# A chunked RWKV-7 recurrence: A turned by plain transpositions, and the transposed inverse turned over by TensorE and copied by ScalarE

## The reference, cut to what matters

```python
def rwkv7_scan(r, decay, k, v, kk, a):
    def step(S, inp):
        r_t, w_t, k_t, v_t, kk_t, a_t = inp
        sa = jnp.einsum('bhij,bhj->bhi', S, -kk_t)
        S = (S * w_t[:, :, None, :] + sa[..., None] * (kk_t * a_t)[:, :, None, :]
             + v_t[..., None] * k_t[:, :, None, :])
        return S, jnp.einsum('bhij,bhj->bhi', S, r_t)
```

## Time and profile before

| | us |
|---|---|
| median of 3 executions | 2356.2 |
| lowest, highest | 2354.84, 2357.73 |
| the profiled execution | 2356.96 |
| its span on the core | 2353.5 |
| outside the span | 3.5 |
| the stage's four pairs, from the first `prod` to the last `y` | about 220 |

### The profile page before, as it was taken

How to read it: one execution, slowest core, us unless ns; L and a number is a source line. 1 busy time by engine, 2 the same in 40 slices (tenths; PEclk the granted TensorE clock), 3 DMA queues, 4 the chain that set the end, 5 groups by cost and what they waited for, 6 DMA issues and landing times.

```text
span 2353.5 us, 36980 instructions
## 1 busy us (share of the span) xinstructions
PE 2300.9 (98%) x13968; PEld 1898.6 (81%) x13968; DVE 1168.3 (50%) x1781; ACT 912.7 (39%) x1448; POOL 1159.2 (49%) x687
## 2 busy tenths in 40 slices
PE   8999999999999999999999999999999999999998
PEld 7888887888888888878766777888888877888887
DVE  5432146268644421376555455713725986731732
ACT  5332225467753321265633264222234435321222
POOL 5444444554565454444644344444445983444442
PEclk9999999999999999999999999999999999999999
DMA  4222323310032332231110112222222232222221
GB/s 165 98 98 98 98 89 109 124 55 1 10 108 98 98 96 93 97 116 63 49 45 29 43 43 91 95 98 98 98 89 92 90 108 81 98 96 92 98 95 57
DMA packets 56126, 200.09 MB, mean 85 GB/s; under 512 B 6224, under 2 KB 6480, under 8 KB 56016
## 3 DMA queue, kind: packets, MB, share of 16 engines
q1 hardware_dynamic: 54432, 195.82, 25.1%
q10 hardware_dynamic: 1584, 2.75, 0.4%
HBM read 196.45 MB, written 2.10 MB: 84 GB/s over the span
## 4 chain that ended last, share of the span: by engine, by line
PE 51%; DVE 3%; ACT 1%; issue 0%; DVEq 0%
PE ps L133 15%; PE ps L134 14%; PE ps L135 14%; PE ps L2048 1%; PE ps L641 1%; PE ps L2024 0%; DVE ps L3084 0%; PE ps L2044 0%; PE ps L656 0%; PE ps L2095 0%; PE ps L1987 0%; DVE sb_ak_lo L1014 0%; PE ps L2009 0%; PE ps L627 0%; PE ps L1916 0%
## 5 line engine op out<-in xcount | busy, mean ns | idle before, releaser
L114 POOL TENSOR_TENSOR sb_w_lo<-sb_w_raw,sb_w_hi 128x1024 fp32r<-128x1024 f32 (+1 forms) x361 | 881.6, 2445 | 948.7 <-ACT sb_w_hi L101 947.3
L133 PE MATMUL ps<-sb_xn_hi,sb_w_hi 128*128 128x512 f32 x1688 | 669.3, 397 | 3.2 <-DVE sb_xn_lo L175 2.8
L135 PE MATMUL ps<-sb_xn_hi,sb_w_lo 128*128 128x512 f32 x1688 | 657.6, 390 | 0.0
L134 PE MATMUL ps<-sb_xn_lo,sb_w_hi 128*128 128x512 f32 x1688 | 657.4, 389 | 0.0
L101 ACT ACTIVATE sb_w_hi<-sb_w_raw 128x1024 fp32r<-128x1024 f32 x362 | 379.8, 1055 | 480.9 <-PE ps L135 454.8
L133 PEld LDWEIGHTS ps<-sb_xn_hi,sb_w_hi 128*128 128x128 f32 x1688 | 316.2, 187 | 75.7 <-issue 4.0
L135 PEld LDWEIGHTS ps<-sb_xn_hi,sb_w_lo 128*128 128x128 f32 x1688 | 316.2, 187 | 67.7 <-issue 0.2
L134 PEld LDWEIGHTS ps<-sb_xn_lo,sb_w_hi 128*128 128x128 f32 x1688 | 316.5, 187 | 65.6 <-issue 2.2
L133 PE MATMUL ps<-sb_hid_hi,sb_w_hi 128*128 128x512 f32 x864 | 336.4, 389 | 2.0 <-DVE sb_hid_lo L401 2.0
L135 PE MATMUL ps<-sb_hid_hi,sb_w_lo 128*128 128x512 f32 x864 | 336.1, 389 | 0.0
L134 PE MATMUL ps<-sb_hid_lo,sb_w_hi 128*128 128x512 f32 x864 | 336.1, 389 | 0.0
(11 more groups left out here) (488 smaller groups left out, 2985.2 us busy)
## 6 DMA issues: line engine op xcount, KB each, us to landing
sb_w_raw<-weights SPq DMA_DIRECT2D x365, 512.0 KB, 3.4
sb_stage<-x SPq DMA_DIRECT2D x4, 512.0 KB, 5.2
out<-sb_out_stage SPq DMA_DIRECT2D x8, 256.0 KB, 2.9
sb_abias<-table ACTq DMA_DIRECT2D x4, 256.0 KB, 5.0
sb_lora_w<-lora ACTq DMA_DIRECT2D x2, 256.0 KB, 2.6
sb_rstd<-table ACTq DMA_DIRECT2D x1, 256.0 KB, 2.6
sb_root<-table ACTq DMA_DIRECT2D x1, 256.0 KB, 4.8
sb_ss<-table ACTq DMA_DIRECT2D x1, 256.0 KB, 5.0
```

The source lines that it names most:

```text
L114: pool.tensor_tensor(c.w_lo[:, slot, 0:width], c.w_raw[:, slot, 0:width], c.w_hi[:, slot, 0:width].bitcast(F32), ALU.subtract).then_inc(c. ...
L133: pe.matmul(out, hi, rhs_hi(k0 + k), start=first, stop=False)
L134: pe.matmul(out, hi, rhs_lo(k0 + k), start=False, stop=False)
L135: mm = pe.matmul(out, lo, rhs_hi(k0 + k), start=False, stop=last)
```

## The change: what it does

- **turnA** becomes 4 plain transpositions like the others. ScalarE swaps the halves in its copy: one copy for the first head, two for the second. The order of turnings becomes V, B, K, A.
- **Levels 1 to 4**: `e0` to `e3` and VectorE's additions `E0` to `E3` go. In their place TensorE turns `D` over (`t1` to `t4`, D against the identity, right after `w`), and ScalarE copies the result to `E` (`turned_back`). `d` of the level now waits for that copy too. The last level keeps `e4` and its addition.
- **Spreading**: VectorE's two copies `recx` and `yrecx` go. `kkb` and `yrb` become 8 matmuls each, one column of norms repeated 64 times as the stationary operand against the whole identity.
- **Order**: `lora_a` moves ahead of `kknorm`, `kknorm` behind `w0`, `var` from level 0 to level 1, `kkb` from level 2 to 3; VectorE's `rec`, `L` and `kk` move one level later. ScalarE's `ysq` goes behind `lv`, and its list becomes: `value`, E1, `root`, `yroot`, E2, `sigw`, E3, `siga`, `ld`, `rks`, E4, then the high parts (for pair 3 the loads of tables and copies that stood ahead of `root`), then `exps`.

The core of the diff:

```diff
-TURN_BANKS = (6, 7, 5, 4)
+TURNS = (("V", 3, 6), ("B", 1, 7), ("K", 2, 5), ("A", 0, 4))
+def by_channel_pe(pe, c, bank, norm):
+
+    for b in range(TT):
+        for s in range(2):
+            mm = pe.matmul(c.ps[HALF[s], bank, b * P:b * P + P], norm[:, 1, b, s:s + 1].broadcast_to([P, HD]), c.ident[:],
+                           start=True, stop=True)
+    return mm
@@ rwkv_pe
-                    mm = pe.transpose(ps[:, TURN_BANKS[x], b * P:b * P + P], sources[x][:, b * P:b * P + P], c.ident[:])
-            done(name, mm)
+                mm = pe.transpose(ps[:, bank, b * P:b * P + P], sources[x][:, b * P:b * P + P], c.ident[:])
+            done("turn" + name, mm)
         prepare(q, "lora_w")
-        prepare(q, "kknorm")
+        prepare(q, "lora_a")
...
             done(f"w{lv}", mm)
             if lv == 0:
+                prepare(q, "kknorm")
+                A(j, "tA")
...
                 done("lv", mm)
-                fill(j, 2)
+            else:
+                for b, s, p in tiles():
+                    mm = pe.matmul(ps[across(s, p), 4 + s, block(b)], w.D[HALF[p], s, b], c.ident_head[HALF[p]], start=True, stop=True)
+                done(f"t{lv}", mm)
+            if lv == 3:
+                prepare(q, "kkb")
+            fill(j, 2 + lv)
+            if lv == 1:
                 tail(t, "var")
-                prepare(q, "lora_a")
-            elif lv == 2:
-                prepare(q, "kkb")
-            if lv >= 1:
-                fill(j, 2 + lv)
             V(j, f"W{lv}")
-            if lv == 0:
-                A(j, "lv")
+            A(j, "lv" if lv == 0 else f"E{lv}")
@@ rwkv_act
+    def turned_back(j, lv):
+
+        E(j, f"t{lv}")
+        done(f"E{lv}", act.activation(w.E[:], parity_banks(ps, 4), ACT.Copy))
...
+            if name == "A":
+                act.activation(w.tok[:, x, :, HALF[0]], turned[:, :, HALF[0]], ACT.Copy)
+                act.activation(w.tok[HALF[1], x, :, HALF[1]], turned[HALF[0], :, HALF[1]], ACT.Copy)
+                op = act.activation(w.tok[HALF[0], x, :, HALF[1]], turned[HALF[1], :, HALF[1]], ACT.Copy)
...
         done("lv", act.activation(heads(w.LV[:]), parity_banks(ps, 4), ACT.Copy))
+        tail(j - 1, "ysq")
         prepare(j + 1, "value")
+        turned_back(j, 1)
+        prepare(j + 1, "root")
+        tail(j - 1, "yroot")
+        turned_back(j, 2)
+        prepare(j + 1, "gates")
+        turned_back(j, 4)
@@ rwkv_act, prepare "gates", between sigw and siga
+            if j >= 1:
+                turned_back(j - 1, 3)
@@ rwkv_dve
-            prepared("recx", dve.tensor_copy(w.tmp2.rearrange("p (x n) -> p x n", n=HD), spread(w.norm)))
-            ended("yrecx", dve.tensor_copy(w.ysq.rearrange("p b (s n) -> p (b s) n", s=2), spread(w.ynorm)))
-            elif lv == 1:
+            elif lv == 2:
                 prepare(q, "rec")
-            elif lv == 2:
+            elif lv == 3:
                 prepare(q, "L")
-            elif lv == 3:
+            elif lv == 4:
                 prepare(q, "kk")
-            E(j, f"e{lv}")
-            done(f"E{lv}", dve.tensor_tensor(Et, Et, banked(4), ALU.add))
+            else:
+                E(j, f"e{lv}")
+                done(f"E{lv}", dve.tensor_tensor(Et, Et, banked(4), ALU.add))
```

More of the change, by code:

```diff
@@ L1598, in rwkv_preparation @@
 def rwkv_preparation():
-    pe = ["lora_w", "kknorm", "lora_a", "kkb", "bonus"]
+    pe = ["lora_w", "lora_a", "kknorm", "kkb", "bonus"]
     act = ["k1", "k2", "r1", "r2", "sq", "v1", "v2", "root", "sigw", "siga", "ld", "rks", "eP", "ePi", "ePp", "ePn", "ePe"]
-    dve = ["raw1", "raw0", "raw2", "rootmax", "rec", "recx", "L", "kk", "bon"]
+    dve = ["raw1", "raw0", "raw2", "rootmax", "rec", "L", "kk", "bon"]
     pool = ["k", "kk0", "r", "v", "ka", "kfin", "rk", "lp", "le", "A", "b0", "B", "K", "Bp", "Kp", "pend", "R"]
@@ L1622, in rwkv_tail @@
 def rwkv_tail():
-    return ["mean", "var", "yrb", "gate"], ["ysq", "yroot"], ["yc", "yrec", "yrecx", "yn", "ysum", "out"]
+    return ["mean", "var", "yrb", "gate"], ["ysq", "yroot"], ["yc", "yrec", "yn", "ysum", "out"]
 PREPARATION = dict(zip(("pe", "act", "dve", "pool"), rwkv_preparation()))
@@ L1917, in prepare @@
         elif part == "kkb":
[L1918 to L1921, removed]
+            PV(j, "rec")
+            if j >= 2:
+                TA(j - 2, "yroot")
+            mm = by_channel_pe(pe, c, b_norm, w.norm)
         else:
             PL(j, "rk")
-            PA(j, "root")
-            if j >= 2:
-                TA(j - 2, "yroot")
+            PV(j, "kk")
             mm = pe.matmul(ps[:, bonus_bank(u, j)], c.ones_head[:], w.rk, start=True, stop=True)
@@ L1946, in tail @@
             if t < PAIRS - 2:
[L1947 to L1950, removed]
+                PA(t + 2, "siga")
+            TV(t, "yrec")
+            mm = by_channel_pe(pe, c, bank, w.ynorm)
         else:
@@ L1963, in rwkv_pe @@
     prepare(0, "lora_w")
+    prepare(0, "lora_a")
     unit_part(1, 0, 1)
     prepare(0, "kknorm")
-    prepare(0, "lora_a")
     unit_part(1, 1, KU + 4)
@@ L2002, in rwkv_pe @@
         sources = (AR[:, 0], w.BKp[:, 0], w.BKp[:, 1], w.v)
[L2003 to L2006, removed]
+        for name, x, bank in TURNS:
+            V(j, "mm1" if bank >= 6 else "dm")
+            if j == 0 and name in ("B", "K"):
+                PL(j, name + "p")
             for b in range(TT):
[L2008 to L2013, removed]
-                    mm = pe.transpose(ps[:, TURN_BANKS[x], b * P:b * P + P], sources[x][:, b * P:b * P + P], c.ident[:])
-            done(name, mm)
+                mm = pe.transpose(ps[:, bank, b * P:b * P + P], sources[x][:, b * P:b * P + P], c.ident[:])
+            done("turn" + name, mm)
         prepare(q, "lora_w")
-        prepare(q, "kknorm")
+        prepare(q, "lora_a")
         for lv in range(len(LEVELS)):
@@ L2021, in rwkv_pe @@
             if lv == 0:
-                A(j, "tV")
+                A(j, "tB")
             for b, s, p in tiles():
@@ L2046, in rwkv_pe @@
                 done(f"d{lv}", mm)
[L2047 to L2050, removed]
+            else:
+                for b, s, p in tiles():
+                    mm = pe.matmul(ps[across(s, p), 4, group(b, s)], w.W[across(s, p), s, b], w.E[across(s, p), s, b],
+                                   start=True, stop=True)
+                done(f"e{lv}", mm)
         fill(j, 7)
```

29 lines of the change are left out of this document (13 added, 16 removed).

## The result

| | before | after |
|---|---|---|
| median, us | 2355.78 | 2365.43 |
| lowest, highest (6 runs each) | 2354.20, 2357.73 | 2363.48, 2366.60 |
| span of the profiled execution | 2353.5 | 2363.2 |
| `ru` of pairs 0 to 3 behind the first turning | 25.85, 32.72, 32.74, 30.53 | 30.47, 34.25, 37.49, 30.99 |

The ratio is 1.0039, 95% interval 1.0028 to 1.0051: the change costs 9.65 us. Forecast were 9.8 and 2366.0.

A forecast was written before the change was run, and what follows sets the result against it. TensorE, busy 98% of the span, bounds it. Pair 0 4.6, pairs 1 and 2 0.9 each, pair 3 0.2, pair 0's kkb and last yrb 0.7 each, clock 1.8: 9.8 us, so 2366.0 us; range 2353.5 to 2373.

The forecast's parts named there:

- Turnings: Ahead of w0: sixteen transpositions save 2.15 us per pair; lora products 2 x 1.06; w0 at 4.07 instead of 6.14.
- Levels: Level 0 takes 4.62 us; levels 1 to 4 take 3.48 instead of 3.02, as t stands where fill covered W.
- The first queue: Pairs 0 to 2: GpSimd's way from late siga to low part, 9.63 us, holds fill 7 until 27.1 or 29.5.
- The second queue, pair 0: ScalarE's high parts and exponentials behind E4 delay u's copy in pair 0; ru at 30.4, 4.6 us later.
- Spreading: kkb and yrb: eight matmuls in 16 passes take 1.05 us, with change of shape 0.7 more than now.
- Rival "series": Spreading's column halves in kkb and yrb work one after another: 2.1 us each, 2372 us in all; chance 0.08.
- The term of 0.7 at pair 0's `kkb`: Pair 0's kkb lies on the path among gapless products: spreading by matmuls costs 0.7 us more there.
- The clock: Half clock follows TensorE's 3 us stand ahead of fill 7: 0.9 us in each of pairs 1 and 2.
- Pair 3: No prepare: w4 0.8 us sooner, t4 takes back 0.5, yrb 0.7; loss 0.2 us, with 1 us either way.
- queues don't bind: Rival: GpSimd goes from siga to low part in time, 6.4 us instead of 9.63; 2353.9 or 2351.1 us; chance 0.22.
- A second collision of GpSimd and VectorE: Late siga puts kfin under L's scan: 0.8 us; 2363.6 without, 2368.4 with two; chance within forecast's 0.60.
- The end: Last yrb, behind the last ru: spreading by matmuls costs 0.7 us more.

The follow-up runs named there:

- e4: Here TensorE's group in the last level, not a run; the run numbered so is the kernel after with levels and ScalarE's list as before: 2349.50 us.
- the swap: Kernel after with siga ahead of E3 instead of behind it on ScalarE's list: 2360.58 us, ratio to before 1.0026.
- e10_pair0_clear: e5_lows_behind_v with pair 0's first two high parts made before the pair and the third behind value: 2353.36 us.
- e1_first_early: Kernel after with only fill 7's first high and low part made before the turnings' copies and GpSimd's wait for siga: 2364.30 us.
- e5_lows_behind_v: Kernel after with fill 7's high parts before the turnings' copies and its three low parts behind GpSimd's v, before siga: 2359.20 us.
- e8_after_mended: e5_lows_behind_v with ScalarE's root and ysq ahead of lv's copy: 2351.34 us.
- e7_root_first: Kernel after with levels and ScalarE's order as before, then root and ysq put ahead of lv's copy: 2338.68 us.
- e12_turnings_old: Kernel after with A turned as before (12 matmuls, one copy) and in the old order: 2371.01 us.

## Why the prediction was right, point by point

**The number stands on a sum whose terms did not all hold.** 9.8 against 9.65, but several terms were off and cancelled. That the number is so close is luck; the direction and the mechanism are not.

*Turnings: the mechanism right, the price too low.* `w0` was to start at T = 4.07 and started at 3.12 in pair 0. The two lora products were summed as 2 x 1.06. Side by side, `lora_w` on partitions 0 to 63 and `lora_a` on 64 to 127, they begin in the same hundredth (1151.58), and `w0` follows 1.05 us later. So the change saves 3.0 us up to `w0` there (6.13 - 3.12), not 2.07 (6.14 - 4.07). In pairs 1 and 2 `lora_a` waits 0.2 us for `yc`, and `w0` is at 3.61, which saves 2.5.

*Levels: right.* Level 0 took 4.64 (4.62), a level 3.50 (3.48), with 0.95 us of bare TensorE ahead of each `w` (0.8 to 1.0). The next level costs more, not less, as worked out: `t` is cheap but stands where there already was cover. `w1` to `w2` with `var` took 5.86 (5.9), the pause ahead of `var` 1.75 (1.5).

*The first queue: right.* `siga` at T = 16.48 (17.4, early by the lora products), 9.58 us from there to the low part (9.63), fill 7 at 26.12 (27.1). In pair 1 19.32 (19.9), 9.59 and 28.96 (29.5). In pair 2, where the clock held `w3` back, `siga` came at 22.48, and 9.57 us later the low part: the way is as long, wherever it begins. That it binds is shown by the swap and by e10_pair0_clear.

*The second queue, pair 0: right by luck in its end.* `u`'s copy began right behind the last exponential (0.12 us idle), 8.95 us behind `w4` (8.9). But TensorE's `u`, behind fill 7 and stretched by the half clock, ended only 0.07 us ahead of that copy: here both queues ended together, and the trace can't tell which of them held it. `w4` was 1.1 us sooner than forecast, at 19.74; `ru` should have followed at 29.3. It came at 30.47 (30.4), since the half clock behind the wait stretched `u` and `z` to 0.95 and 0.99 and `z`'s copy came late. The prediction had written that the half clock would hide in pair 0. It did not.

*Spreading: right.* 16 passes took 1.02 us (1.05) at full clock: the two halves of the columns work at once. Rival "series" is out. The term of 0.7 at pair 0's `kkb` was hidden by what the lora products gained ahead of it (`kkb` began 0.92 us sooner, the group behind it 0.45), so the start moved by -0.45.

*The clock: the step that failed.* It was to halve behind fill 7 only, 0.9 us in each of pairs 1 and 2. Pair 1 did so. Pair 2, with the same list, had it twice. Granted clock is the third number from the end, PE's busy time the second number; the first row is pair 1 behind `var`, the second pair 2 at the same place:

```profile
1217.80:1222.00 4.20, 3.38 (x132) 2.62 (x131) 1.66 (x4) 1.71 (x3) 0.00 (x0) 1.00 0.00 0
1279.00:1283.00 4.00, 3.21 (x80) 2.78 (x75) 1.66 (x4) 0.80 (x2) 0.00 (x0) 0.50 0.02 4
```

Both come behind a pause of 1.75 us. From `w1` to `w3` pair 2 took 11.70 and pair 1 9.35, and `w3` to `w4` 5.83 and 4.98: 3.2 us, all of what pair 2 lost beyond pair 1's 1.53. The forecast of 1.8 for each held in pair 1 and was 3 us short in pair 2. What failed is the step by which the half clock follows a pause of 3 us and not one of 1.5. The prediction's reading that pair 2 repeats pair 1 within 0.1 us holds for `ru` alone: in the kernel before `w1` came at T = 15.33 in pair 1 and 15.82 in pair 2, and both reached `w2` at 19.8.

*Pair 3: right* (+0.46, forecast +0.2; its own three terms, -0.8, +0.5 and +0.7, add up to 0.4). *The rivals:* "queues don't bind" gave 6.4 us for the point that decides, and 9.58 was measured. A second collision of GpSimd and VectorE did not come: `kfin` took 2.05 us under the scan, as `rk` had before, one collision for one. `w` and `t` together took 1.09 us by their loads (1157.27 to 1158.36; 1.08 forecast), so `t` isn't the 1.05 of `e`.

*The end.* Behind the last `ru` 0.7 us more were forecast and 1.2 less came. In the kernel before, 40 us behind pair 3's `ru`, a group of 20 matrix loads ran in part at the half clock and took 3.94 us; in the kernel after the same group took 2.37. The busy times of these stretches, before and then after (clock third from the end), and the group after:

```profile
1390.00:1395.00 5.00, 4.17 (x21) 4.16 (x22) 2.73 (x6) 4.31 (x14) 5.00 (x6) 0.66 0.39 117
```

```profile
1402.00:1407.00 5.00, 4.28 (x31) 4.13 (x32) 3.21 (x8) 4.82 (x14) 5.00 (x5) 1.00 0.39 118
...
1402.69 2.37 PEld L641 LDWEIGHTS ps<-sb_y,sb_later_p 128*128 128x128 f32 x20 [2.11 <-DVE sb_later_pt_lo L792]
```

Its code is untouched, and both stood for 2.11 us ahead of it. So 1.57 us of the difference are the clock again, this time in favour of the kernel after.

The sum then reads, forecast against measured: the start 0.7 and -0.45, pairs 0 to 3 together 8.4 and 11.36 (nearly all of the excess in pair 2), between them 0 and -0.04, the end 0.7 and -1.2. Three us too many and three too few met. Each alone would have left the result inside the range.

## What to carry to other kernels

An operation given to an idle engine is not free if it stands ahead of something on that engine's list: read who waits for what is queued behind it, here `siga`, GpSimd, and a low part that TensorE needs 10 us later. Ahead of moving work, ask which turn of a loop is bare and which is covered; a cheaper operation moved out of the bare turn makes the loop longer. And when an experiment ends where the rival said, look at the trace before believing it: two of these ended there by a collision of their own.

## What the hardware showed that was not expected

- Two fp32 products with 64 rows each, one on either half of the partitions, ran side by side: both in 1.05 us, where one alone took 1.06.
- A VectorE sum with both operands in SBUF, begun 0.02 us behind a GpSimd subtraction, took 2.87 us instead of 0.68 (e1_first_early). The same engine's additions with one operand in PSUM took 0.69 beside the same GpSimd work (e5_lows_behind_v).
- The granted clock halved without any pause of over 1 us. In e8_after_mended, pair 1, TensorE was busy for 2.19 and 2.48 of 3 us, in waits of at most 0.95 by its loads, and then the clock fell; in e7_root_first it was busy throughout and the clock stayed:

```profile
1212.00:1215.00 3.00, 2.19 (x99) 1.69 (x97) 0.91 (x2) 1.69 (x3) 1.20 (x2) 1.00 0.00 0
1215.00:1218.00 3.00, 2.48 (x57) 2.13 (x47) 0.93 (x2) 0.87 (x2) 3.00 (x2) 1.00 0.02 5
...
1219.00:1220.00 1.00, 1.00 (x45) 0.99 (x39) 0.63 (x2) 0.00 (x0) 1.00 (x2) 0.50 0.92 369
```

- Whether it halves behind the same pause differs between pairs of one execution, as pairs 1 and 2 show, and between kernels: behind 3.4 us ahead of fill 7 in pair 0 it was 0.71 in the kernel after and 1.00 in e12_turnings_old. Why is open; no run here was made to settle it. It makes a kernel whose TensorE stands often hard to price: 3 us here hung on it.
